# First loads of a long single-core kernel: smaller transfers in order of use, constants already laid out as columns, and the c rows and modulation weights behind x

## The reference, cut to what matters

```python
# first block: the first thing computed
x = x + 0.5 * swiglu(rms_norm(x, ffn1_norm), ffn1_w_gu, ffn1_w_down)
#   ffn1_w_gu: 2048 x 11264 (gate and up), ffn1_w_down: 5632 x 2048
...  # norm, w_in, attention, w_out, a second swiglu, norm
# second block, two layers: three modulation vectors of width 2048
# for c and for c_ctx, used only much later
mod = silu(c) @ w_mod[l] + b_mod[l]      # w_mod: 2 x 2048 x 6144
```

## Time and profile before

| | us |
|---|---|
| median of three runs | 3328.55 |
| lowest and highest | 3326.57, 3329.41 |
| the profiled execution, its own time | 3330.59 |
| its span in the profile | 3328.8 |
| PE busy in the span | 3263.6 (98%) |
| DVE busy | 2272.5 (68%) |
| ACT busy | 1552.5 (47%) |

### The profile page before, as it was taken

One profiled execution on the slowest core, in us unless ns is written; L12 is line 12 of the kernel. 1 busy time (PEld: TensorE's weight loads), 2 busy tenths in 40 slices (PEclk: granted clock), 3 DMA queues, 4 the chain that ended last, 5 costly groups with the idle time before them and its releaser, 6 DMA issues.

```text
span 3328.8 us, 40638 instructions
## 1 busy us (share of the span) xinstructions
PE 3263.6 (98%) x15142; PEld 2647.6 (80%) x15142; DVE 2272.5 (68%) x4132; ACT 1552.5 (47%) x2872; POOL 91.1 (3%) x174
## 2 busy tenths in 40 slices
PE   9999999999999999999999999999999998999998
PEld 7888888888888788888888788888867776888766
DVE  7888887876776788888777533557565436746665
ACT  6544454546665555545555422222265335422464
POOL 0000000000000000000000000000000000000000
PEclk9999999999999999999999999999999999999999
DMA  8888887776455788888787432333312335533524
GB/s 277 262 269 260 259 259 261 250 248 201 148 152 177 263 259 258 262 266 264 256 267 246 133 91 87 97 96 102 98 58 89 101 98 169 178 109 101 168 88 154
DMA packets 285316, 614.21 MB, mean 185 GB/s; under 512 B 18688, under 2 KB 21312, under 8 KB 283456
## 3 DMA queue, kind: packets, MB, share of 16 engines
q1 hardware_dynamic: 261792, 527.50, 49.7%
q0 software_dynamic: 21952, 80.69, 7.6%
q10 hardware_dynamic: 1376, 3.44, 0.3%
HBM read 605.26 MB, written 6.29 MB: 184 GB/s over the span
## 4 chain that ended last, share of the span: by engine, by line
PE 90%; DVE 4%; ACT 3%; DMA 2%; issue 1%; SPq 0%; ACTq 0%; DVEq 0%
PE acc L426 28%; PE acc L428 28%; PE acc L427 28%; DVE lo L421 1%; PE tp L2381 1%; PE acc L2402 1%; ACT hi L417 1%; PE acc L2367 1%; PE tp L2340 1%; PE tp L1977 1%; DMA raw<-ffn_w_gu 1%; ACT pr L1047 0%; PE cgw L2352 0%; PE cgw L2113 0%; PE tp L1939 0%
## 5 line engine op out<-in xcount | busy, mean ns | idle before, releaser
L417 ACT ACTIVATE hi<-raw 128x512 fp32r<-128x512 f32 x1808 | 1132.8, 631 | 1537.5 <-PE acc L428 1475.2
L421 DVE TENSOR_TENSOR lo<-raw,hi 128x512 fp32r<-128x512 f32 x1808 | 1209.2, 689 | 862.8 <-ACT hi L417 854.9
L426 PE MATMUL acc<-hi,hT_hi 128*128 128x512 f32 x1760 | 700.0, 398 | 23.8 <-DVE hT_lo L1206 7.9
L428 PE MATMUL acc<-lo,hT_hi 128*128 128x512 f32 x1760 | 686.2, 390 | 0.0
L427 PE MATMUL acc<-hi,hT_lo 128*128 128x512 f32 x1760 | 686.2, 390 | 0.0
L426 PE MATMUL acc<-hi,h_hi 128*128 128x512 f32 x1696 | 671.2, 396 | 10.0 <-DVE lo L421 6.6
L428 PE MATMUL acc<-lo,h_hi 128*128 128x512 f32 x1696 | 662.1, 390 | 0.0
L427 PE MATMUL acc<-hi,h_lo 128*128 128x512 f32 x1696 | 661.5, 390 | 0.0
L426 PEld LDWEIGHTS acc<-hi,hT_hi 128*128 128x128 f32 x1760 | 330.6, 188 | 115.2 <-DVE hT_lo L1206 13.7
L428 PEld LDWEIGHTS acc<-lo,hT_hi 128*128 128x128 f32 x1760 | 330.8, 188 | 69.7
L427 PEld LDWEIGHTS acc<-hi,hT_lo 128*128 128x128 f32 x1760 | 331.0, 188 | 68.1 <-issue 2.6
(11 more groups left out here) (283 smaller groups left out, 2166.8 us busy)
## 6 DMA issues: line engine op xcount, KB each, us to landing
raw<-ffn_w_gu SPq DMA_DIRECT2D x352, 512.0 KB, 5.8
raw<-w_in SPq DMA_DIRECT2D x280, 512.0 KB, 3.8
raw<-ffn_w_down SPq DMA_DIRECT2D x176, 512.0 KB, 5.3
mw<-wmt POOLq DMA_DIRECT2D x132, 512.0 KB, 5.5
raw<-w_out SPq DMA_DIRECT2D x96, 512.0 KB, 4.2
mw<-wmt SPq DMA_DIRECT2D x60, 512.0 KB, 6.0
ball<-rpbx SPq DMA_DIRECT2D x8, 768.0 KB, 10.7
x<-x_rest SPq DMA_DIRECT2D x2, 2048.0 KB, 7.6
```

What stands on the lines that cost most here:

```text
L417: act.activation(hi[:, g % RING, :], raw_piece(g), ACT.Copy).then_inc(S["hi_made"], 1)
L421: dve.tensor_tensor(lo[:, g % RING, :], raw_piece(g), hi[:, g % RING, :].bitcast(F32), ALU.subtract).then_inc(S["lo_made"], 1)
L426: pe.matmul(bank, act_hi, hi[:, slot, :], start=start, stop=False)
L428: return pe.matmul(bank, act_hi, lo[:, slot, :], start=False, stop=stop)
```

## The change

- x chunk 0 is loaded in two halves of 256 columns (256 KB each). Units 0 and 1 are loaded in gate and up halves (256 KB each). SP's order becomes: first half of x chunk 0, gate of unit 0, gate of unit 1, second half of x chunk 0, up of unit 0, up of unit 1, units 2 and 3, x chunk 1, and so on; the later x chunks stand two units later than before.
- ACT and DVE take the first half of x before pieces 0 and 1, and the second half after them. PE runs 3, 2 and 4 fills where it ran 4 and 6.
- The constants come from memory already as columns, by DMA straight into `vec`, `bmod`, `cvec` and `dw`. The transposes and copies of `vrow`, `brow` and `drow` are gone.
- The four transfers of c and c_ctx are issued by POOL once x chunk 3 is in, ahead of the modulation weights; the two Silu of `cb` move from lap 0 to lap 1. The 256 KB of `ogc` (a gain used much later) is loaded behind all of these instead of first.
- Lap 0 has no modulation part. The remaining ten laps hold 60, d1 holds 36, and POOL loads all 96 of layer 0. Layer 1 is as before.

```diff
--- before.py
+++ after.py
@@ -253,7 +250,9 @@
-        D_MODS = tuple(1 + 84 * n // 29 for n in range(MODS - 6 * FC))
+        GU_FIRST = (1, 0)
+        GU_PARTS = [6 * (FC - first) for first in GU_FIRST]
+        D_MODS = [tuple(1 + 84 * n // (MODS - made - 1) for n in range(MODS - made)) for made in GU_PARTS]
@@ -410,7 +409,9 @@
             u, half = spot(g)
-            if half == 0:
+            if g < 2:
+                act.wait_ge(S[f"head{u}"], 16)
+            elif half == 0 or g < 4:
                 act.wait_ge(S[f"raw{u % RING}"], 16 * (u // RING + 1))
@@ -528,9 +529,8 @@
-            ly, m = divmod(n, MODS)
-            return (f"modg{n % 2}", 16 * (3 * FC * ly + m // 2 + 1)) if m < 6 * FC else \
-                (f"modd{n % 2}", 16 * ((MODS // 2 - 3 * FC) * ly + m // 2 - 3 * FC + 1))
+            k = n - MODS - GU_PARTS[1]
+            return (f"modg{n % 2}", 16 * (n // 2 + 1)) if k < 0 else (f"modd{n % 2}", 16 * (k // 2 + 1))
@@ -550,20 +550,20 @@
-            def load_gu(w, ph, x_before={}):
+            def load_gu(w, ph, begun=0, x_before={}):
                 for i in range(FC):
-                    for u in range(16):
+                    for u in range(0 if i else begun, 16):
                         if i == 0 and u in x_before:
-                            x_load(x_before[u])
+                            x_load(f"x_in{x_before[u]}", x_before[u] * CH, CH)
                         unit(ph.pieces // 2 + 16 * i + u, w[i, u])
-            def load_down(w, ph, mod):
+            def load_down(w, ph, ly):
                 for i in range(4):
...
                         unit(ph.pieces // 2 + 22 * i + u, w[i, u])
-                        if 22 * i + u in D_MODS:
-                            mod_load(sp, mod + D_MODS.index(22 * i + u))
+                        if ly and 22 * i + u in D_MODS[ly]:
+                            mod_load(sp, MODS * ly + GU_PARTS[ly] + D_MODS[ly].index(22 * i + u))
@@ -581,12 +581,20 @@
-            def x_load(c):
-                sp.dma_start(x1[:, :, c * CH:(c + 1) * CH], x_v[:, :, c * CH:(c + 1) * CH]).then_inc(S[f"x_in{c}"], 16)
-
-            x_load(0)
-            load_gu(gu[0], phases["g1"], {2: 1, 4: 2, 6: 3})
-            load_down(down[0], phases["d1"], 6 * FC)
+            def x_load(name, d0, n):
+                sp.dma_start(x1[:, :, d0:d0 + n], x_v[:, :, d0:d0 + n]).then_inc(S[name], 16)
+
+            def half_unit(u, half, name):
+                sp.dma_start(raw[:, u, half * CH:(half + 1) * CH], gu[0][0, u][:, half]).then_inc(S[name], 16)
+
+            x_load("x_in0", 0, L)
+            half_unit(0, 0, "head0")
+            half_unit(1, 0, "head1")
+            x_load("x_in0b", L, L)
+            half_unit(0, 1, "raw0")
+            half_unit(1, 1, "raw1")
+            load_gu(gu[0], phases["g1"], 2, {4: 1, 6: 2, 8: 3})
+            load_down(down[0], phases["d1"], 0)
             for k, c in enumerate(ORDER):
@@ -645,23 +653,14 @@
                 act.dma_start(ident[:], a["ident"]).then_inc(S["const_in"], 16)
-                act.dma_start(vrow[:], a["vrows"]).then_inc(S["const_in"], 16)
+                act.dma_start(vec[:], a["vcols"]).then_inc(S["vec_in"], 16)
...
-                act.dma_start(brow[0:96, :], a["b_mod_2"].rearrange("l (k p) -> (l k) p", p=P)).then_inc(S["rows_in"], 16)
-                for k, nm_ in enumerate(("conv_dw_b_2", "conv_ln_g_2", "conv_ln_b_2")):
-                    act.dma_start(brow[96 + 8 * k:104 + 8 * k, :],
-                                  a[nm_].rearrange("l (k p) -> (l k) p", p=P)).then_inc(S["rows_in"], 16)
-                for ly in range(2):
-                    act.dma_start(drow[:, ly, :],
-                                  a["conv_dw_2"][ly].rearrange("k (c p) -> (k c) p", p=P)).then_inc(S["rows_in"], 16)
-
-            def c_rows():
-
-                for h in range(2):
-                    act.dma_start(cb[h][:, 0], row_bc(a["c_2"][0:1, h * KH:(h + 1) * KH], KH)).then_inc(S["c_raw"], 16)
-                    act.dma_start(cb[h][:, 1], row_bc(a["c_ctx_2"][h * KH:(h + 1) * KH], KH)).then_inc(S["c_raw"], 16)
+                act.dma_start(bmod[:], a["rcols"][:, 0:96]).then_inc(S["rows_in"], 16)
+                act.dma_start(cvec[:], a["rcols"][:, 96:120]).then_inc(S["rows_in"], 16)
+                act.dma_start(dw[:, :, 0:124], a["rcols"][:, 120:368].rearrange("p (l n) -> p l n", l=2))\
+                   .then_inc(S["rows_in"], 16)
@@ -671,9 +670,9 @@
-            def x_hi(ph, v, c):
-
-                for f in range(2):
+            def x_hi(ph, v, c, halves=(0, 1)):
+
+                for f in halves:
                     act.wait_ge(S["tp_done"], ph.groups + 2 * c + f + 1)
@@ -730,8 +729,7 @@
                         hi_piece(act, ph.pieces + 32 * c + j)
-                        if c == 0:
-                            extra(j)
+                        extra(32 * c + j)
                         if c and j in (7, 9):
@@ -749,20 +747,19 @@
             consts()
-            for j in range(LOOK):
-                hi_piece(act, j)
-            act.wait_ge(S["cols_taken"], 3)
-            x_hi(phases["n1"], 0, 0)
+            act.wait_ge(S["vec_in"], 16)
+            x_hi(phases["n1"], 0, 0, (0,))
+            hi_piece(act, 0)
+            hi_piece(act, 1)
+            x_hi(phases["n1"], 0, 0, (1,))
             def first_lap(j):
-                if j in (4, 10, 18):
-                    x_hi(phases["n1"], 0, 1 + (4, 10, 18).index(j))
-                if j == 2:
-                    c_rows()
-                if j == 3:
+                if j in (7, 10, 18):
+                    x_hi(phases["n1"], 0, 1 + (7, 10, 18).index(j))
+                if j == 13:
                     row_consts()
-                if j in (8, 12):
-                    h = (8, 12).index(j)
+                if j in (36, 44):
+                    h = (36, 44).index(j)
                     act.wait_ge(S["c_raw"], 64)
@@ -1234,8 +1232,8 @@
                             u_lo(c - 1, (8, 10).index(j))
-                        if j > 8 and (j - 3) // 2 in GU_MODS and j % 2:
-                            mod_part(MODS * ly + 6 * c + GU_MODS.index((j - 3) // 2))
+                        if c >= GU_FIRST[ly] and j > 8 and (j - 3) // 2 in GU_MODS and j % 2:
+                            mod_part(MODS * ly + 6 * (c - GU_FIRST[ly]) + GU_MODS.index((j - 3) // 2))
                     for t in range(2):
@@ -1255,8 +1253,8 @@
                         m, odd = divmod(DK * c + j - 3, 2)
-                        if not odd and m in D_MODS:
-                            mod_part(MODS * ly + 6 * FC + D_MODS.index(m))
+                        if not odd and m in D_MODS[ly]:
+                            mod_part(MODS * ly + GU_PARTS[ly] + D_MODS[ly].index(m))
                         after(c, j)
@@ -1289,27 +1287,18 @@
-            dve.memset(ones[:], 1.0).then_inc(S["cols_taken"], 1)
-            dve.memset(dw[:], 0.0).then_inc(S["cols_taken"], 1)
-            dve.wait_ge(S["cols_taken"], 2)
-            dve.wait_ge(S["cols_made"], 1)
-            dve.tensor_copy(vec[:], acc[0][:, 0:NV]).then_inc(S["cols_taken"], 1)
-            for j in range(LOOK):
-                lo_piece(dve, j)
-            dve.wait_ge(S["cols_taken"], 3)
-            x_lo(phases["n1"], 0, 0)
-
-            def rows_take():
-                dve.wait_ge(S["cols_made"], 2)
-                for dst, c0, c1 in ((bmod[:], 0, 96), (cvec[:], 96, 120), (dw[:, 0, 0:124], P, P + 124),
-                                    (dw[:, 1, 0:124], 2 * P, 2 * P + 124)):
-                    dve.tensor_copy(dst, tp[0][:, c0:c1]).then_inc(S["cols_taken"], 1)
+            dve.memset(ones[:], 1.0).then_inc(S["consts_set"], 1)
+            dve.memset(dw[:], 0.0).then_inc(S["consts_set"], 1)
+            dve.wait_ge(S["consts_set"], 2)
+            dve.wait_ge(S["vec_in"], 16)
+            x_lo(phases["n1"], 0, 0, (0,))
+            lo_piece(dve, 0)
+            lo_piece(dve, 1)
+            x_lo(phases["n1"], 0, 0, (1,))
             def first_lap(j):
-                if j in (4, 10, 18):
-                    x_lo(phases["n1"], 0, 1 + (4, 10, 18).index(j))
-                if j == 25:
-                    rows_take()
+                if j in (7, 10, 18):
+                    x_lo(phases["n1"], 0, 1 + (7, 10, 18).index(j))
                 if j == 26:
@@ -1952,9 +1941,9 @@
-                if ready:
-                    ready()
                 for f in range(2):
+                    if ready:
+                        ready(f)
                     wait(pe, "tg_lo", ph.groups + 2 * c + f - 1 if c else ph.groups)
@@ -2049,34 +2036,29 @@
-            pe.wait_ge(S["cols_taken"], 2)
+            def x_in(c):
+                return lambda f: None if f else pe.wait_ge(S[f"x_in{c}"], 16)
+
+            def first_x(f):
+
+                if f:
+                    fill(acc[3], 2)
+                pe.wait_ge(S[("x_in0", "x_in0b")[f]], 16)
+
+            pe.wait_ge(S["consts_set"], 2)
+            fill(acc[3], 3)
```

(59 more changed lines are left out.)

## The result

Over 20 runs of each kernel in turn the changed one takes 3335.62 us in the median, the one before 3329.93; the ratio is 1.0016 with a 95% interval of 1.0009 to 1.0022. Forecast were 3322.2 us and a range up to 3327. The profiled execution took 3337.06 us, its span is 3335.2.

The account below looks back on a forecast made before the run. PE was taken to bound the kernel behind lap 0, so only lap 0 could gain. The terms, 2.7 + 1.7 + 2.5 - 0.4 - 0.1 = 6.4 us, gave 3322.2 us, range 3319 to 3327.

Parts of the forecast that it names:

- Term 1: Start of lap 0: the first product starts at 9.5 us instead of 12.21, a gain of 2.7 us.
- Term 2: Start of lap 0: PE's clock is already up at the first product, a gain of 1.7 us.
- rival of a low clock: Start of lap 0: the clock stays low, the gain is only 3.5 us, 3325.1 us; chance 2 in 10.
- Term 3: Lap 0: PE's gaps at unit 4, the modulation parts and the transposes go, a gain of 2.5 us together.
- Term 4: Lap 0: POOL's c and `mw` transfers slow the weight units; 0.4 us lost, between 0 and 1.2.
- Term 5: d1: six more modulation parts on DVE and loads moved to POOL; 0.1 us lost, between 0 and 1.
- slower side: d1: `mw` loaded from POOL's queue lands late and holds DVE and PE; 3336 us, chance 4 in 100.

Follow-up runs that it names:

- b_d1_pool: The kernel before, with its 30 layer 0 parts in d1 loaded from POOL's queue instead of SP's; 3326.76 us, ratio 0.9989.
- a_d1_sp: The changed kernel, with the 36 layer 0 parts in d1 loaded from SP instead of POOL; 3333.25 us, ratio 1.0004 to the kernel before.
- h_paced_even: The changed kernel, with c transfers paced by PE's used pieces and the 36 d1 parts at even units; 3321.62 us, ratio 0.9972 to the kernel before.
- j_rows2k: The changed kernel, with c transfers written as eight of 512 columns instead of four of 1024; 3335.80 us, ratio 1.0017 to the kernel before.
- d_rows_late: The changed kernel, with the three transfers of constants in columns issued at piece 50 instead of 13; 3334.79 us, ratio 1.0011 to the kernel before.

## Why the prediction was wrong

- **Term 1, the start: right.** 9.5 us was forecast, 9.53 came. The second half of x was turned from 7.50 us on, after a wait for its landing, inside the 6.9 to 7.8 us given. Two misses cancel in it: 6.9 was taken and 7.50 came, and from there to the product it was 2.03 us, where 2.5 had been counted.
- **Term 2, the clock: right.** It is 1.00 from 8 to 18 us. The rival of a low clock did not come at the start; a low clock came behind the new gaps.
- **Term 3, the gaps of lap 0: right.** None of them is left.
- **Term 4, what comes back in lap 0: mis-sized.** 0.4 us was put down, 1.2 at most. Units took 11 to 12 us to land instead of the forecast 6 to 8. In the profiled executions d1 begins at 502.6 to 508.0 us in the seven kernels that have c transfers together behind x, most of them near 505, and at 501.3 and 500.2 in the two that have them paced: about 4 us, of which some 1.7 can be the clock behind the gap. The step at fault was the shortfall of bytes against a slack of 2.6 us: it gave SP's queue a third of the rate all through the burst, 3.8 us short in all. The third held from 31 to 37 us (0.76 of 2.37 MB), but from 25 to 31 us SP's queue had 0.09 MB of 1.58. So the unit of 25.34 us was 5.5 us later than the usual 5.5, 2.9 beyond the slack, and the gap was priced without the clock behind it.
- **Term 5, d1: the step that turned the sign.** "In laps 1 to 10 parts stand every four pieces and PE still has 0.31 us idle; in d1 they will stand every four or six" compared distances alone. It missed that a part's place within four pieces decides whether it delays the loads (36 parts behind even units 242.4 us, behind odd ones 273.0), and that `D_MODS` with 36 entries puts runs of three behind odd units. 0.1 us was put down, 7.9 came. Beside terms 1 to 4 this makes the kernel slower.
- **The rivals.** The slower side was given 4 in 100 and for another reason: `mw` late from POOL's queue. DVE did not wait for `mw` in d1, and b_d1_pool shows that the move of 30 parts costs PE nothing; so the Trainium skill's rule on loads issued from GpSimd (SBUF — State Buffer, section SBUF: two separate sides) does not show itself here: `mw` landed after 5.4 us in the median in the changed kernel's d1, as it did in a_d1_sp from SP. That section ties the delay to VectorE instructions in its 2-port modes; the prediction's "just these loads" said more than it does, and no run shows whether the instructions of d1 are of that kind. With the mixed plan d1 took 251.0 to 254.3 us from POOL in four kernels and 247.6 us from SP in one; that the queue adds these 3 to 7 us to a bad phase is likely, from one profile of SP, but how it does is open.
- **An aside.** The prediction says that 0.5 us between 64 and 512 KB agrees with the slope of the Trainium skill (DMA: Bandwidth & Descriptors, section Anatomy of one DMA), 436 GB/s. It does not: 448 KB at that rate are 1.05 us, an estimate. The section gives its fit for transfers issued from GpSimd, and x comes from SP's queue. Nothing in the sum rested on it.
- **The sum.** The gain holds for the change without its two faults: h_paced_even has the front of the change and takes 3321.62 us, where 3322.2 was forecast. That closeness is partly luck. The forecast started from a kernel before of 3328.6 us, and beside h_paced_even it took 3330.72, so the gain is 9.1 us (5.7 to 12.7 by the interval of the ratio) and not 6.4. In the profiles 7.3 us of it are there when d1 begins, and 0.7 more come from d1, which with even units takes less than before.

## What to carry to other kernels

When side work is put between the steps of a ring, ask which step of the group releases the next loads and put it behind that step; equal distances in another phase are not the same plan, and here late releases two units apart likely added up. A burst of transfers beside a ring has to be priced by how late the first unit behind it lands, as a gap plus the lower clock seen after it here; pacing the transfers by the consumer's own count costs five waits, in three lines. Whether a variant varied what it was meant to vary can be read in its own profile, as the packets of j_rows2k show. A gain at the front only counts if what was moved out of its way lands in a place with room.

## What the runs showed that was not expected

- ACT's table load can come onto the path. In the changed kernel it runs when the first half of x has been turned, 1.28 us on the way to `h_hi`. Before, it ran at 1.74 us, long ahead of the first ACTIVATE, which waited for weights until 8.35 us. Both loads stand at the line of the first ACTIVATE; why one waited and the other did not is open. Before, then after:

```profile
1.74 1.28 ACT L417 ACT_TABLE_LOAD   x1 [1.74 <-issue]
```

```profile
5.00 1.28 ACT L679 ACT_TABLE_LOAD   x1 [5.00 <-PE tp L1951]
6.30 0.84 ACT L679 ACTIVATE h_hi<-tp,vec 128x256 fp32r<-128x256 f32 x2
```

  PE's fills covered it this time.
- In the changed kernel the granted clock was 0.65 and 0.50 in 38 to 40 and 40 to 42 us, behind 1.98 us of idle of PE, and 0.62 in 62 to 64 us, behind 1.95 us. In d_rows_late 1.52 us of idle ended at 36.73 us, and the granted clock was 1.00 from 36 to 42 us. After the gaps of d1 in the changed kernel, up to 1.7 us of idle, the slowest product took 0.504 us, where products at the low clock took 0.63.
